# Paired experts of the first block: the four unread products at the end of each step are left out

## The reference

```python
def expert(xb, g, e):
    hb = jax.nn.silu(xb @ w_exp_gate[e]) * (xb @ w_exp_up[e])
    return (hb @ w_exp_down[e]) * g[:, None]
```

## Time and profile before

| | before |
|---|---|
| median of 3 runs | 1964.89 us |
| lowest, highest | 1961.93, 1966.2 us |
| profiled execution: span from the first to the last instruction | 1960.0 us |
| what lies around the span (median less span; no time is given for the profiled execution alone) | 4.9 us |
| TensorE matrix products, busy | 1791.1 us, 91% |
| TensorE weight loads, busy | 1151.2 us, 59% |
| VectorE, ScalarE, GpSimd, busy | 1007.4, 781.5, 560.3 us |
| `keep_clock` products (L1173), whole program | 178 records, 90.9 us busy |
| mean granted TensorE clock | 0.961 of full speed |

### The profile page before, as it was taken

How to read it: one execution, slowest core, us unless ns; L and a number is a source line. 1 busy time by engine, 2 the same in 40 slices (tenths; PEclk the granted TensorE clock), 3 DMA queues, 4 the chain that set the end, 5 groups by cost and what they waited for, 6 DMA issues and landing times. The chain is left out here.

```text
span 1960.0 us, 24773 instructions
## 1 busy us (share of the span) xinstructions
PE 1791.1 (91%) x7962; PEld 1151.2 (59%) x7962; DVE 1007.4 (51%) x1976; ACT 781.5 (40%) x1404; POOL 560.3 (29%) x435
## 2 busy tenths in 40 slices
PE   6989999989999959999999699899999999999992
PEld 3434446754333337776788575677666766666661
DVE  1866416431111036632633354777767777677673
ACT  2412217311111135633632122566655655565551
POOL 4997807011111118801100000222222322222221
PEclk9789999989999979999999899999999999999996
DMA  5353410668999853222022444599999999999873
GB/s 193 129 182 108 172 43 5 247 253 335 406 406 403 340 165 130 87 87 92 1 86 101 162 184 155 206 342 339 337 327 321 337 333 339 328 325 328 324 249 108
DMA packets 116829, 441.71 MB, mean 225 GB/s; under 512 B 27428, under 2 KB 31924, under 8 KB 79368
## 3 DMA queue, kind: packets, MB, share of 16 engines
q1 hardware_dynamic: 93672, 406.94, 55.1%
q0 software_dynamic: 23040, 33.64, 7.4%
q10 hardware_dynamic: 32, 0.04, 0.0%
HBM read 438.34 MB, written 55.11 MB: 252 GB/s over the span
## 5 line engine op out<-in xcount | busy, mean ns | idle before, releaser
L1885 DVE TENSOR_TENSOR big_parts<-big,h_cols_parts 128x1024 fp32r<-128x1024 f32 x256 | 305.7, 1221 | 48.0 <-ACT h_cols_parts L1938 41.0
L2149 POOL DMA_INDIRECT acc_scratch<-heads,small x80 | 131.4, 1642 | 530.3 <-DVE small L1916 303.8
L1938 ACT ACTIVATE h_cols_parts<-big 128x1024 fp32r<-128x1024 f32 x256 | 262.7, 1060 | 27.7 <-PE bank L1844 24.5
L1875 PE MATMUL bank<-big,heads 128*128 128x512 f32 x512 | 236.1, 604 | 0.8 <-ACT heads L1946 0.8
L1842 PE MATMUL bank<-h_cols_parts,heads_parts 128*128 128x512 f32 x512 | 205.5, 401 | 2.2 <-DVE heads_parts L1905 2.2
L1844 PE MATMUL bank<-h_cols_parts,heads_parts 128*128 128x512 f32 x512 | 200.2, 391 | 0.0
L1843 PE MATMUL bank<-big_parts,heads_parts 128*128 128x512 f32 x512 | 199.3, 389 | 0.0
L1875 PEld LDWEIGHTS bank<-big,heads 128*128 128x128 f32 x512 | 92.5, 190 | 93.3 <-issue 92.3
L458 PE MATMUL bank<-big,h_cols 128*128 128x512 f32 x320 | 144.7, 607 | 0.3 <-ACT heads L608 0.3
L1971 ACT ACTIVATE heads<-bank 128x512 f32<-128x512 f32 x64 | 38.3, 599 | 237.8 <-DMA acc_scratch<-heads,small 201.8
L1842 PEld LDWEIGHTS bank<-h_cols_parts,heads_parts 128*128 128x128 f32 x512 | 96.7, 189 | 20.2 <-DVE heads_parts L1905 2.5
(11 more groups left out here) (430 smaller groups left out, 3353.3 us busy)
## 6 DMA issues: line engine op xcount, KB each, us to landing
big<-in_w_exp_gate_dram SPq DMA_DIRECT2D x86, 1024.0 KB, 17.6
big<-in_w_exp_up_dram SPq DMA_DIRECT2D x86, 1024.0 KB, 25.7
big<-in_w_exp_down_dram SPq DMA_DIRECT2D x72, 1024.0 KB, 18.2
big<-in_w_in_dram SPq DMA_DIRECT2D x13, 2048.0 KB, 8.8
junk_and_spare<-in_w_mod_dram SPq DMA_DIRECT2D x24, 1024.0 KB, 5.3
x_res<-in_w_exp_down_dram SPq DMA_DIRECT2D x16, 1024.0 KB, 18.1
big<-in_w_out_dram SPq DMA_DIRECT2D x4, 2048.0 KB, 9.0
h_rows<-in_w_exp_down_dram SPq DMA_DIRECT2D x8, 1024.0 KB, 21.0
```

What stands on the lines that cost most here:

```text
L1875: mm = pe.matmul(b_y[half][:, :], hidt[:, b, P * j:P * j + P], dn[q][:, j, 512 * half:512 * half + 512], start=j == 0, stop=j == FH - 1)
L1885: dve.tensor_tensor(gu_low[q][:, :, part, :], gu[q][:, :, part, :], gu_high[:, :, part, :].bitcast(F32), ALU.subtract).then_inc(w_low, 1)
L1938: act.activation(gu_high[:, :, part, :], gu[q][:, :, part, :], ACT.Copy).then_inc(w_high, 1)
L2149: return pool.indirect_dma_start(out=K.acc_dram, out_offset=bass.IndirectOffsetOnAxis(at, 0), in_=rows, in_offset=None, bounds_check=S - 1 ...
```

## The change

The two last lines of TensorE's step are taken out, so that steps 1 to 15 end with the down products. The other calls of `keep_clock` stay, among them the one a few lines above in the first steps.

```diff
@@ -1555,8 +1555,6 @@
                                 mm = pe.matmul(b_y[half][part, :], hidt[:, b, P * j + HALF * n:P * j + HALF * n + HALF],
                                                dn[places[n]][:, j, 512 * half:512 * half + 512], start=j == 0, stop=j == FH - 1)
                     mm.then_inc(y_mm, 1)
-                    if has(i, 0):
-                        keep_clock(K, pe, b_ht, 4)
 
         @block.vector
         def _(dve):
```

## The result

| | before | after the change |
|---|---|---|
| median (20 runs each) | 1965.18 us (1960.48 to 1968.99) | 1969.22 us (1962.06 to 1974.34) |
| ratio, with 95% interval | | 1.0022 (1.0013 to 1.0030) |
| profiled execution: span; its own time | 1960.0 us; not given | 1965.6 us; 1967.36 us |
| TensorE matrix products, busy | 1791.1 us | 1757.5 us |
| records of TensorE's products (two for each 32-bit product) | 7962 | 7842 |

The change made the kernel slower by 0.22%, some 4 us. I had forecast no change (1965.1 us, 1959 to 1969) and gave "slower" 11%. The median lies just outside the range and the interval of the ratio leaves out 1, so the forecast was wrong.

A forecast was written before the change was run, and what follows sets the result against it. DMA transfers were taken to pace the stage. 0 us in steps 1 to 14 and +0.2 us at its end made the span 1960.0 into 1960.2 us; with 4.9 us up to the median, 1965.1 us, range 1959 to 1969 us.

The forecast's parts named there:

- slower: Whole kernel: clock not coming back (3% whole, 3% in part) or earlier requests disturbing transfers or the end (5%); 11% together.
- Transfers pace the stage: Paired experts' stage: DMA transfers set 17.7 to 17.9 us per pair, independent of TensorE, hidden for nine steps by early loads.
- Value 0 in steps 1 to 14: Steps 1 to 14: removed groups gain 0 us, since weight landings do not move; bounds 1 us loss, 3.5 us gain.
- Waits in 11 steps, 35 to 60 us: Sign of being right: TensorE waits for gate and up weights in about 11 steps, some 35 to 60 us in all.
- The clock: Most steps from pair 5 on: cold starts cost 1.7 us, at most 2.9, hidden by DMA waits except in step 15.
- The end of the stage: Step 15 to last addition: 1.5 us gain, of it 1.4 through the additions, less 1.7 cold start: 0.2 us loss.
- The term for the cold start: Step 15: TensorE starts cold after waiting some 2 to 4 us before pair 15, costing 1.7 us on the path.
- It adds nothing, moves no DMA issue and adds no wait: The change itself: only removes 15 groups of four products, 53.0 us of TensorE, with no other effect.
- later stages keep their times: Sign of being right: stages behind the changed one take the same time as before.
- The 4.9 us that I put around the span: Whole kernel: 4.9 us between profiled span and median, added to the span of 1960.2 us.
- the bounds as I gave them: Whole kernel: a gain of 3.5 + 1.5 us, a loss of 1 + 1.4 us, about 2 us either side for scatter.

The follow-up runs named there:

- late_kept: Kernel before with the groups of unread products gone in steps 1 to 8 only, kept in steps 9 to 15; ratio 1.0029 (1.0015 to 1.0043).
- ten_gone: Kernel before with the groups of unread products gone in steps 1 to 10, kept in 11 to 15; one execution, 1975.85 us.
- tiny: Kernel before with all 15 groups keeping their four products, but 8 columns in place of 512; ratio 0.9997 (0.9982 to 1.0012).
- tiny_second: Repeat: kernel before with four products of 8 columns in place of 512 in every group; ratio 0.9996 (0.9985 to 1.0007).
- filler_best: Kernel before, groups replaced by 60 products of 8 columns in steps 1 to 14 (five in steps 2 to 5, else four), none in 15; ratio 1.0001.
- pad4: Kernel before, all groups kept, with four more products of 8 columns in step -1; ratio 1.0016 (1.0002 to 1.0029).
- pad4_inside: Kernel before, all groups kept, with four more products of 8 columns at the end of step 5; ratio 1.0020 (1.0010 to 1.0030).
- again: The change once more, all 15 groups gone, against the kernel before; ratio 1.0016 (0.9998 to 1.0034).
- third: The change measured a further time, all 15 groups gone, against the kernel before; ratio 1.0017 (1.0008 to 1.0026).
- moved_pad: The change with 60 products of 8 columns added at the end of step 2 alone; ratio to the kernel before 1.0074 (1.0058 to 1.0090).
- pad32: Kernel before, all groups kept, with 32 more products of 8 columns in step -1; ratio 1.0062 (1.0046 to 1.0077).

## Why the prediction was wrong

- *Transfers pace the stage*: right. The last load landed 0.4 us from where it had (241.9 us after the first gate and up products, 242.7 before), doubled groups set the pace with steps of 19.11 us, longer than the 17.8 of the transfers, and removing the groups of steps 1 to 8 moved nothing.
- *Value 0 in steps 1 to 14*: right, for steps 1 to 10 by late_kept and ten_gone (263.0 us each) and for all by the times of tiny, tiny_second and filler_best.
- *Waits in 11 steps, 35 to 60 us*: right, 11 waits, 42.7 us.
- *The clock*: it dips, and the dips are hidden. tiny shows the same for a whole run. The Trainium skill, page "TensorE: Matmul & The Clock Gate", section "HAM oscillation — how this bites in real kernels", counts the penalty of the cold clock as extra wall time, 19 us here as the prediction estimated it. It does not hold in this stage, where the landing paces the step: the ratios of tiny, tiny_second and filler_best are 0.9997, 0.9996 and 1.0001.
- *The end of the stage*: the mechanism was right, the additions hand on 1.4 us of 3.5 (6.55 us apart in place of 7.98). The term for the cold start had no place in it: I took a cold step 15 with a net loss of 0.2 us after a wait of 2 to 4 us, but TensorE had waited only 1.6 us before pair 15, its gate and up products took 7.09 us, and the gain stayed. Stages with all groups gone average 261.5 us over six traces, those of before and with 16 records more 262.6 over five: 1.1 us. Single traces of one program lie up to 3 us apart here (260.8 to 263.8 for the change), so I take the 1.1 us, by that spread, as an estimate good to some half a microsecond.
- *"It adds nothing, moves no DMA issue and adds no wait"* and *"later stages keep their times"*: here the prediction failed. It put every stage behind this one at nothing, without a reason, and so left out what 240 missing records do to the code behind them. The term is the second jump of TensorE's queue, 3.45 to 3.87 us in five traces at this place and 0.33 to 0.35 in all twelve others. From its start to the first instruction of the last norm it is 7.5 to 8.1 us against 4.2 to 5.3, on average 7.75 and 4.62, so 3.1 us of it lie on the path. pad4 and pad4_inside bring it about with nothing removed (1.0016, 1.0020), tiny, tiny_second and filler_best take it away with everything else of the change kept (0.9997, 0.9996, 1.0001).

With this term the sum is 3.1 - 1.1 = +2 us, 0.10%. The three measurements of the change say 0.16 to 0.22%, 3 to 4 us. The intervals of again and third hold 0.10%, that of the 20 runs begins at 0.13%. Something of 1 to 2 us stays unexplained; I could not place it, and the scatter of single traces is larger.

Two numbers of the sum were off besides, and neither changes the account. The 4.9 us that I put around the span are 1.7 to 2.0 us in every execution that has both its time and its span on record; the rest was that the profiled execution was a fast one of its kernel. And the bounds as I gave them, a gain of 5 and a loss of 2.4 us with 2 us to either side, make 1958 to 1969.3 us around 1964.9, not 1959 to 1969: the measured 1969.22 us lies at this upper edge by the allowance for scatter, not by anything that the sum had foreseen.

Why this jump is slow at some places is shown in part. That it hangs on fetched pieces of the program is borne out by four observations:

- Queue q8 fetches TensorE's program in pieces of 16 KB (0.80 MB in 49 packets on the page of either kernel). In the trace of before, TensorE goes through 5429 records, waits included, between its first fetch and the 22nd, some 259 to a fetch, and 16 KB over 256 records is 64 bytes for each. The four kernels whose program is longer than before have 50 fetches, all others 49.
- Slow and short jumps repeat with the shift taken modulo 256: -240 is as +16, -128 as +128, +240 as -16.
- In each of the eight slow jumps a fetch of q8 ends 1.3 to 1.5 us before the jump does. In the short ones the fetch starts at the same distance (1.1 us behind the start of the second jump, 3.3 to 3.8 behind the first), but the queue has gone on before.
- The slow first jump is the longer one because its fetch starts 3.6 to 3.9 us after the jump, while loads run, and that of the slow second jump 1.0 to 1.1 us after it.

The Trainium skill states the rule outright, page "Runtime: NRT & Kernel Launch", section "Instruction fetch mechanics": instructions come in blocks of 16 KiB or 256 instructions, prefetched in sequence only, and a taken branch to a target outside the current two blocks waits for a DMA fetch. The traces agree with the block and with the wait for a fetch; that the window is two blocks no run here tests. It fits the code: the skipped stages have four and three lists of tokens, each with some 84 records of products and weight loads of TensorE, so at least 336 and 252 without the waits and the loop's own instructions, about one block or more. (The 420 and 312 of the expectation of ten_gone counted a transpose as four records; it leaves two. With fewer the slow places are fewer too, so that its forecast for the first jump was less sure than it sounded, though it held.) So whether a jump leaves the window depends on where in its block it starts. That section, laid beside the two jumps in the trace of before, gives the rival that was missing: both jumps are short there, and by that rule a shift of the code can only leave them so or make them longer.

## What to carry to other kernels

A change in the length of an engine's program is a change in itself where that queue later jumps over a skipped stage. After adding or removing unrolled instructions, compare the compare-and-branch rows of every queue, before reading any engine's time. To tell an instruction's time from its place, keep the count and shrink the work (tiny), then keep the work and shift the count (pad4). And work that fills idle time of an engine in a stage paced by transfers can go or stay at no cost, as long as it does not hold back the point that the next loads wait for (moved_pad: 16 us).

## What was not expected of the hardware

- One compare-and-branch of TensorE's queue takes 0.33 to 0.47 us or 3.45 to 6.50 us by its place alone. The slow first jump (6.11 to 6.50 us) stands while weights for the next stage are being loaded, the slow second one (3.45 to 3.87 us) while nothing but instructions is fetched.
- A product of 128 by 128 by 8 columns in 32-bit form costs 0.22 us at the full granted clock (the first ones of the rows in moved_pad and pad32; 0.23 us in the groups of four of tiny) and 0.43 us at a granted 0.50, against 0.88 us for 512 columns in the unread groups (3.53 us for four). In a long row of them the granted clock falls to 0.50 while TensorE is busy without a gap: from 480 us on in moved_pad, from 441 us on in pad32. A busy engine does not mean a full clock.
- Executions of one unchanged program differ by up to 5 us in a stage 700 us long (the second experts stage in the three traces of the change: 696.5, 695.7 and 691.3 us), which is more than the whole effect.
